# First pairs of parts on VectorE, a six-chunk part first, squares on ScalarE, and output remainders off GpSimd

## What is computed

```python
def rmsnorm(x, g):
    y = x32 * lax.rsqrt(jnp.mean(x32 * x32, axis=-1, keepdims=True) + NORM_EPS)
    return (y * g).astype(x.dtype)

def swiglu(h, w_in, w_out):
    a, b = jnp.split(h @ w_in, 2, axis=-1)
    return (jax.nn.silu(a) * b) @ w_out

x = x + 0.5 * swiglu(rmsnorm(x, g_ffa), w_ffa_in, w_ffa_out)
```

## Time and profile before

| | us |
|---|---|
| median of 3 runs | 2741.33 (2737.09 to 2744.72) |
| the profiled execution | 2743.89 |
| its span, first to last instruction | 2742.2 |
| mean granted TensorE clock | 0.963 |

### The profile page before, as it was taken

One profiled execution on the slowest core, in us unless ns is written; L12 is line 12 of the kernel. 1 busy time (PEld: TensorE's weight loads), 2 busy tenths in 40 slices (PEclk: granted clock), 3 DMA queues, 4 the chain that ended last, 5 costly groups with the idle time before them and its releaser, 6 DMA issues.

```text
span 2742.2 us, 45352 instructions
## 1 busy us (share of the span) xinstructions
PE 2528.1 (92%) x17541; PEld 2395.5 (87%) x17541; DVE 1713.1 (62%) x2326; ACT 1023.4 (37%) x1707; POOL 694.6 (25%) x416
## 2 busy tenths in 40 slices
PE   4999998999899899999997999998999989999988
PEld 4999988876688899898986989898987889898978
DVE  6827367788554883645778637278334696372786
ACT  4525242344233352433234425252134244252422
POOL 2040322212330503223232140503322321405032
PEclk9999999999899999999998999999999999999998
DMA  3323223122232133222222323233323223232322
GB/s 98 92 77 92 83 83 81 41 50 78 67 111 60 54 93 90 79 82 79 80 66 72 92 72 97 62 91 79 93 54 97 81 77 93 76 92 62 91 72 65
DMA packets 410793, 216.25 MB, mean 79 GB/s; under 512 B 40085, under 2 KB 407834, under 8 KB 410650
## 3 DMA queue, kind: packets, MB, share of 16 engines
q1 hardware_dynamic: 404646, 209.17, 27.4%
q0 software_dynamic: 3584, 1.84, 0.4%
q10 hardware_dynamic: 2420, 3.37, 0.4%
HBM read 206.57 MB, written 7.76 MB: 78 GB/s over the span
## 4 chain that ended last, share of the span: by engine, by line
PE 71%; DVE 14%; issue 5%; POOL 5%; ACT 4%; DMA 1%; DVEq 0%; SPq 0%; ACTq 0%; POOLq 0%
PE ps L2431 11%; PE ps L2433 11%; PE ps L2432 11%; PE ps L2374 9%; PE ps L2379 9%; PE ps L2376 9%; PE ps L995 2%; DVE x L2193 1%; DVE st L613 1%; DVE xh L2080 1%; PE ps L909 1%; POOL g2f L1753 1%; POOL wlo L1740 1%; DVE ub L2191 1%; DVE r L2059 1%
## 5 line engine op out<-in xcount | busy, mean ns | idle before, releaser
L1729 POOL TENSOR_TENSOR wlo<-raw,whi 128x1024 fp32r<-128x1024 f32 (+2 forms) x175 | 404.4, 2311 | 1648.8 <-ACT whi L1804 1648.8
L1804 ACT ACTIVATE whi<-raw 128x1024 fp32r<-128x1024 f32 (+2 forms) x175 | 169.5, 968 | 534.6 <-PE ps L2379 509.9
L2374 PE MATMUL ps<-uh,whi 128*128 128x320 f32 (+1 forms) x1408 | 304.5, 298 | 17.8 <-DVE x L2193 10.9
L2376 PE MATMUL ps<-ul,whi 128*128 128x320 f32 (+1 forms) x1408 | 302.8, 296 | 0.0
L2379 PE MATMUL ps<-uh,wlo 128*128 128x320 f32 (+1 forms) x1408 | 302.7, 296 | 0.0
L2191 DVE TENSOR_TENSOR ub<-ps,r 128x576 f32<-128x576 f32 x96 | 72.5, 755 | 298.1 <-PE ps L2379 298.1
L2374 PEld LDWEIGHTS ps<-uh,whi 128*128 128x128 f32 x1408 | 217.3, 190 | 21.9 <-ACT whi L1804 15.7
L2116 DVE TENSOR_TENSOR wlo<-raw,whi 128x1024 fp32r<-128x1024 f32 x76 | 101.0, 1329 | 191.9 <-ACT whi L1820 191.9
L2376 PEld LDWEIGHTS ps<-ul,whi 128*128 128x128 f32 x1408 | 217.3, 190 | 0.0
L2379 PEld LDWEIGHTS ps<-uh,wlo 128*128 128x128 f32 x1408 | 217.2, 190 | 0.0
L2374 PE MATMUL ps<-xh,whi 128*128 128x320 f32 x752 | 167.0, 304 | 16.2 <-DVE xl L2073 8.4
(11 more groups left out here) (430 smaller groups left out, 7394.4 us busy)
## 6 DMA issues: line engine op xcount, KB each, us to landing
raw<-in_w_ffa_in SPq DMA_DIRECT2D x88, 512.0 KB
raw<-in_w_ffb_in SPq DMA_DIRECT2D x88, 512.0 KB
raw<-in_w_ffa_out SPq DMA_DIRECT2D x32, 512.0 KB
pages<-in_cache_ckv SPq DMA_DIRECT2D x128, 128.0 KB, 2.0
raw<-in_w_ffb_out SPq DMA_DIRECT2D x32, 512.0 KB
raw<-in_w_mlstm_in SPq DMA_DIRECT2D x24, 512.0 KB
raw<-in_w_ple_gate SPq DMA_DIRECT2D x16, 512.0 KB
raw<-in_w_ffa_out SPq DMA_DIRECT2D x16, 384.0 KB
```

The lines of the kernel that those rows point to most:

```text
L1729: pool.tensor_tensor(lo[:, 0:n, :], raw[:, p % RAW, 0:n, :], hi[:, 0:n, :].bitcast(F32), ALU.subtract).then_inc(wlo_ready, 1)
L1804: act.activation(hi[:, 0:n, :], raw[:, p % RAW, 0:n, :], ACT.Copy).then_inc(whi_ready, 1)
L2374: mm(out[:, t], hi[:, n, :], xh_n[:, t], start=first and n == 0, stop=False)
L2376: mm(out[:, t], hi[:, n, :], xl_n[:, t], start=False, stop=False)
```

## The change

- `PARTS` becomes 6, 8 and 8 pairs.
- Pair 0 of every part is prepared like the others, by VectorE with `second_sums`, `third_sums` and the four `_lower` functions, placed between the output tiles of the part before (tiles 4, 5 and 6 of `ffn_out`), between the mixer's tiles, the ple's chunks or the chunks of the start. ScalarE's uppers move accordingly. GpSimd's `first_pair` and the semaphores `first_sum` and `first_lo` go.
- Of the output panels, GpSimd makes the remainders of 0 and 1; VectorE those of 2 to 7, in `ffn_out`, behind each tile.
- In the last part ScalarE makes `xh` (a scaled copy) and the squares; VectorE makes `xl` and `acc`.
- In the blocks of x ScalarE scales x (into `xTf` or `xBh`), and VectorE's subtractions multiply by the gain themselves; `gneg` holds negated gains.
- TensorE's output tile waits for the reading of the tile two before (`out_read`) instead of its addition to x.
- The silu of an FFN's pair 0 goes behind the first copy of pair 1; at the start the five squares go between the copies of pair 0.

```diff
-PARTS = [(0, 8), (8, 16), (16, 22)]
+PARTS = [(0, 6), (6, 14), (14, 22)]
...
             def ffn(f):
                 for part in PART[f]:
-                    first_pair(part)
-                    for k in range(8):
+                    for k in (0, 1):
                         lower(part.p + k, 0, part.n)
...
+            def gate(part, i):
+                g = part.g0 + i
+                act.wait_ge(w_act, 2 * g + 2)
+                if g:
+                    act.wait_ge(w_ub, g)
+                act.activation(sA[:, :], tA[:, :], ACT.Silu).then_inc(silu_done, 1)
...
                         copied(part, i, 1, 1, B, A)
+                        if i == 1 and part.q == 0:
+                            gate(part, 0)
...
                     upper(part.p + 1, 0, part.n)
-                    for k in range(2, 8):
-                        upper(part.p + k, 0, part.n)
                     if part.q < 2:
-                        first_pair(PART[f][part.q + 1])
+                        after = PART[f][part.q + 1]
+                        for k in range(2, 8):
+                            if k == 7:
+                                second_upper(after, 0)
+                                third_upper(after, 0)
+                            upper(part.p + k, 0, part.n)
+                        fourth_upper(after, 0)
+                        first_upper(after, 0)
                     else:
-                        upper(part.p + 8, 0, last_upper)
+                        for k in range(8):
+                            if k < 6:
+                                upper(part.p + 2 + k, 0, part.n)
+                            elif k == 6:
+                                upper(part.p + 8, 0, last_upper)
+                            act.wait_ge(tile_taken, part.t + k + 1)
+                            x_scaled_upper(nxt, k)
+                            x_squares(nxt, k)
...
+            def x_scaled_upper(name, c):
+                g = gn[:, GCOL[name] + c:GCOL[name] + c + 1]
+                dst = xh2 if name[0:3] == "ple" else xh
+                act.activation(dst[:, c, :], x[:, c, :], ACT.Copy, scale=g).then_inc(xh_act, 1)
...
+            def panel_lower(p, n):
+                hi, lo = whi[:, p % SPLIT, :, :], wlo[:, p % SPLIT, :, :]
+                dve.wait_ge(wlo_ready, p - 8)
+                dve.wait_ge(whi_ready, p - 7)
+                dve.tensor_tensor(lo[:, 0:n, :], raw[:, p % RAW, 0:n, :], hi[:, 0:n, :].bitcast(F32),
+                                  ALU.subtract).then_inc(wlo_ready, 1)
...
+                for c in range(NC_D):
+                    dve.wait_ge(panel_used, part.p + c + 1)
+                    dve.wait_ge(tile_taken, part.t + c)
+                    dve.tensor_tensor(ub[:, :], slot(part.t + c, bank), r[:, :], ALU.mult).then_inc(out_read, 1)
+                    dve.wait_ge(out_read, NC_D * part.k + c + 1)
+                    dve.scalar_tensor_tensor(out=x[:, c, :], in0=ub[:, :], scalar=-0.5, in1=x[:, c, :], op0=ALU.mult,
+                                             op1=ALU.add).then_inc(tile_taken, 1)
+                    if c < 6:
+                        panel_lower(part.p + 2 + c, part.n)
+                    if name:
+                        if c:
+                            x_sum(name, c - 1)
+                        dve.wait_ge(tile_taken, part.t + c + 1)
+                        x_scaled_lower(name, c)
+                    if c == 4 and after:
+                        second_sums(after, 0)
+                        third_sums(after, 0)
+                    if c == 5 and after:
+                        second_lower(after, 0)
+                        third_lower(after, 0)
+                    if c == 6 and after:
+                        fourth_lower(after, 0)
+                        first_lower(after, 0)
...
+            def x_second(f, k):
+                dve.wait_ge(x_lo, 16 * f + k + 1)
+                dve.scalar_tensor_tensor(out=xTf[:, k, 2, :], in0=x[:, 4 + k, HT:T], scalar=g, in1=xTf[:, k, 2, :],
+                                         op0=ALU.mult, op1=ALU.subtract).then_inc(x_f, 1)
...
             def added(name, f):
                 clear_acc()
+                part = PART[f][0]
                 for c in range(NC_D):
...
                     x_blocks(f, c)
+                    if c == 5:
+                        second_sums(part, 0)
+                        third_sums(part, 0)
+                    if c == 6:
+                        second_lower(part, 0)
+                        first_lower(part, 0)
+                third_lower(part, 0)
                 for k in range(4):
                     x_third_lower(f, k)
+                fourth_lower(part, 0)
...
+                    part = PART[2][0]
+                    second_sums(part, 0)
+                    third_sums(part, 0)
+                    first_lower(part, 0)
+                    second_lower(part, 0)
                     blocks_of(7, p0 + 15, t0 + 17)
+                    third_lower(part, 0)
...
-                    with pe.Fori(0, NC_D // 2) as i:
+                    out_tile(0, 0, lambda n: pe.wait_ge(u_ready, part.g0 + n + 1))
+                    out_tile(1, 0)
+                    with pe.Fori(1, NC_D // 2) as i:
                         for k in (0, 1):
-                            pe.wait_ge(tile_taken, part.t + k - 1 + i * 2)
+                            pe.wait_ge(out_read, NC_D * part.k + k - 1 + i * 2)
+                            out_tile(k, i * 2)
```

More of the change, by code:

```diff
@@ L148, in hybrid_step @@
         gn = whole.put("gn", [P, NG])
+        gneg = whole.put("gneg", [P, 4, 4])
         cf = whole.put("cf", [P, NCF])
@@ L1644, in load @@
                     sp.dma_start(dst, src).then_inc(raw_ready[s], inc)
-            def pair_load(part, i, v):
-                h = 2 * part.half(i)
-                for s in (0, 1):
-                    col = s * FF + (part.a + i) * P
-                    sp.dma_start(raw[:, h + s, :, :], v[:, :, col:col + P]).then_inc(raw_ready[h + s], UNIT)
-            def lowered(part, i):
-                if i:
-                    sp.wait_ge(g_lo, part.remainders(i, 4))
-                else:
-                    sp.wait_ge(first_lo, part.lowered(0, 4))
             def ffn(f, w_in, w_out):
@@ L1662, in ffn @@
                         h = 2 * part.half(i)
[L1663 to L1671 removed]
+                        if f == 0 and part.q == 0 and i == 0:
+                            continue
+                        if i >= 2:
+                            sp.wait_ge(g_lo, part.lowered(i - 2))
+                        for s in (0, 1):
+                            last = max([p for p in range(8, part.p) if p % RAW == h + s], default=0)
+                            if i < 2 and last:
+                                sp.wait_ge(wlo_ready, last - 7)
+                            col = s * FF + (part.a + i) * P
+                            sp.dma_start(raw[:, h + s, :, :], vi[:, :, col:col + P]).then_inc(raw_ready[h + s], UNIT)
                     for k in range(8):
@@ L1861, in ffn @@
                         A, C, B, D_ = [ps[:, part.bank(i) + k, 0:HT] for k in range(4)]
+                        embed = not part.k and not i
                         if i:
@@ L2128, in fourth_lower @@
             def fourth_lower(part, i):
-                dve.wait_ge(g_hi, 4 * (part.g0 + i) + 4)
+                dve.wait_ge(g_hi, part.uppers(i, 4))
                 dve.tensor_tensor(blocks(g4l), raw_pair(part, i)[:, 3, :], blocks(g4h).bitcast(F32),
@@ L2475, in pair @@
                     touch(b + 1)
-                pe.wait_ge(g_hi, 4 * g + 3 + dyn * 4)
-                if first and not e:
-                    pe.wait_ge(first_lo, part.lowered(0, 3))
-                else:
-                    pe.wait_ge(g_lo, part.remainders(e, 3) + dyn * 4)
+                pe.wait_ge(g_hi, part.uppers(i, 3) + add)
+                pe.wait_ge(g_lo, part.remainders(i, 3) + add)
                 pe.wait_ge(w_copied, 4 * g + 1 + dyn * 4)
                 block_product(g3h[:, e, :, :], g3l[:, e, :, :], 0, lambda n: xTh[:, n, 2, :], lambda n: xTl[:, n, 2, :], B,
-                              False, False, need(5, 2))
+                              False, False, need(6, 2))
                 block_product(whi[:, s, :, :], wlo[:, s, :, :], 4, lambda n: xBh[:, n, 0:HT], lambda n: xBl[:, n, 0:HT], A,
-                              False, True, need(6, 2))
+                              False, True, need(5, 2))
                 if new and f:
@@ L2492, in pair @@
                               False, True)
-                pe.wait_ge(g_hi, 4 * g + 4 + dyn * 4)
-                if first and not e:
-                    pe.wait_ge(first_lo, part.lowered(0, 4))
-                else:
-                    pe.wait_ge(g_lo, part.remainders(e, 4) + dyn * 4)
+                pe.wait_ge(g_hi, part.uppers(i, 4) + add)
+                pe.wait_ge(g_lo, part.remainders(i, 4) + add)
                 pe.wait_ge(w_copied, 4 * g + 4 + dyn * 4)
```

303 lines of the change are left out of this document (129 added, 174 removed).

## The result

The changed kernel took 2570.68 us (median of 4 runs, 2569.43 to 2572.78) against 2741.33, a ratio of 0.938 (95% interval 0.936 to 0.940): 170.7 us less. The direction and most of the mechanisms named held; the size was short by 21 us, and the step that failed is the tile time of 6.40 us that I carried over unchanged.

A forecast was written before the change was run, and what follows sets the result against it. TensorE, busy 92%, was taken as the bound, with only its 214 us idle and low-clock stretches winnable. Gains of 81 + 36 + 33 = 150 us from 2743.9 gave 2594, as a median 2592, range 2572 to 2632.

The forecast's parts named there:

- the clock against which all must fit: Output tiles: 6.40 us for eight chunks and 4.80 for six, the time into which all VectorE work must fit.
- the ends: Ends of the four networks: 39.6 us lost before; short part first and work on ScalarE gain 36 us.
- first pairs of parts 1 and 2: Eight places: preparing the pair under the previous part's last tiles saves 10.1 us each, 81 us.
- starts, silu moved: Network starts: the reciprocal comes earlier and the silu of pair 0 moves, together 33 us gained.
- remainders of panels 2 to 7: Output tiles: moving these from GpSimd to VectorE gains nothing by itself, covered by VectorE's slack.
- the margins in the six-chunk part: Part 0's last tiles: panel 7's remainder ends 1.4 us early, the pair's last at 7T + 4.3, 0.5 us early.
- the queue at the starts: Two networks behind a mixer: VectorE's queue puts the reciprocal 17.0 us after the last mixer tile, 7.1 gained each.
- more comes back: Rival, chance 0.06: preparing pair 1 lies in gaps of VectorE's queue at three starts, 19 us more, 2573.
- Pair 0's raw slots come free when panels 4 and 5 are lowered: Loads for the next part's first pair: slots free at 3T + 2.8 and 4T + 2.8, in time for the sums.
- my third rival: Chance 0.03: the next pair's raw lands late, VectorE stands at the sums; 18.8 us late makes 2742, no change.
- The rule against it: Skill advice to move work off a saturated VectorE (84% busy in the first end window); tiles would end later.
- the moved silu: Behind pair 1's first copy, it moves TensorE's wait one product on: 0.7 us gained per network.

The follow-up runs named there:

- a_late: Changed kernel with VectorE preparing the first pairs of parts 1 and 2 only behind the last tile of the part before: 2654.07 us.
- a_pool: Changed kernel with the remainders of output panels 2 to 7 back on GpSimd: 2580.77 us.
- a_start: Changed kernel, first pair of the two networks behind a mixer prepared after the last mixer tile's blocks of x, not between the mixer's tiles: 2578.65 us.
- a_silu: Changed kernel with the silu of each network's pair 0 back behind pair 0's last copy: 2574.47 us.
- b_uh64: Kernel before with an unused tile of 64 bytes per partition between xl and uh: 2730.59 us.
- b_pad64: Kernel before with an unused tile of 64 bytes per partition behind gn: 2724.48 us.
- a_f3: Changed kernel; in the fourth network only, panel 0's upper goes behind the last pair's last copy and the next pair 0's sums one tile later: 2561.36 us.
- a_best: Changed kernel; in the fourth network only, panel 0's upper goes behind the last pair's third copy and the next pair 0's sums one tile later: 2558.84 us.

## Where the prediction held, and which step fell short

The measured 2570.68 us lies below the range. The step that failed is "the clock against which all must fit": a tile's time was taken as the same before and after, so that the place of the operands had no term. It is worth 10.6 to 14.3 us of the 21; the ends, under-sized by 8, come next.

| step | predicted | measured |
|---|---|---|
| first pairs of parts 1 and 2 | 81 | 82: 20.2, 20.8 and 20.0 in the first three networks, 20.3 predicted (the fourth counted as the second); 82.8 lost in `a_late` |
| network ends | 36 | 44: 10.9, 11.3 and 10.7 in the first three |
| starts, silu moved | 33 | about 37: 11.9 at the very start, 2 x 6.4, 6.9 to 8.7, and 4.8 inside the networks |
| remainders of panels 2 to 7 | 0 | 8.5 to 9.5 if taken back (`a_pool`), already in the rows above |
| place of the operands in SBUF | not seen | 10.6 to 14.3 |
| fourth network, raw late | not seen | -8.5: 13.3 us over the second network (7.6 before ScalarE's upper, 4.8 in the tiles, 1.0 of half clock), 4.8 before |

82 + 44 + 37 + 12.5 - 8.5 = 167, within 4 us of the two measurements, 170.7 and 167.4 (2738.73 - 2571.32).

- **Right: first pairs.** The time behind the last tile, its half clock and the margins in the six-chunk part (0.6 us where I had 0.5) came as worked out. The margin was partly luck: my own terms, added again, put the last remainder at about 7T + 4.6, not 4.3, which leaves 0.2 us.
- **Right: the queue at the starts.** 17.7 us behind the last mixer tile for 17.0; `a_start` shows that the preparation does not lie in gaps. So my second rival, "more comes back", had the size (2573) but not the mechanism: it was that gaps would hide the preparation of pair 1.
- **Wrong: "the clock against which all must fit".** I took a tile's 6.40 us as the same before and after, in every stage. The diff has a new tile, `gneg`, 64 bytes in front of nearly all operands, and I read it as a VectorE matter. It moved the matmuls' moving operands by 64 bytes and took 3 to 4 ns from the spacing of each 320-column one, start to start. A six- or eight-chunk tile became shorter by 0.06 or 0.08 us, 10.6 to 14.3 us in all. This step had no term at all; it is more than half of the 21 us.
- **Wrong in size: the ends.** I took what TensorE lost as idle time and clock from the earlier trace rows. For the second network the windows gave 10.2 us lost. By the tile starts the same short part took 50.59 us against 38.87, 11.7 lost, of which a later reciprocal gives back 0.4. I think that the windows count matmuls as work that are stretched, but did not test it. And of the 3.6 us that I let remain, the tiles show nothing. The way to measure such a loss is by intervals of the product, not by an engine's busy time.
- **Wrong: the raw slots.** "Pair 0's raw slots come free when panels 4 and 5 are lowered" holds in three networks. In the fourth they are 5 and 6, and my third rival (raw late, 0.03) came true there, at 4.4 us in the six-chunk part. The larger share, ScalarE's wait for panel 0 inside the last pairs, was in no rival. I had checked one network and multiplied by four.
- **Put at nothing: the remainders.** I looked for a wait of TensorE for GpSimd in the kernel before, found none among the costly ones and wrote 0. In the new order GpSimd would be late in the six-chunk part (13.6 us of waits against 3.5), so moving them is a condition of the rest, worth 8.5 to 9.5 us.
- **Small, and right by luck: the pair with the reciprocal.** I gave the moved silu 0.7 us a network, and `a_silu` lost 3.2 for all. But at full clock it is 0.17 each. The second and third network gained 1.7 and 1.6, because the half clock behind the stop inside pair 1 went (below).
- **The rule against it.** "Perfetto Trace Analysis" of the Trainium skill, "Optimizing Scalar/DVE Operations", says that with VectorE saturated it may make sense to move some of its work to ScalarE or even GpSimd. I left out that it goes on to say that GpSimd might not help, as the two share a read port. The trace fits both halves: `xh` and the squares went to ScalarE, GpSimd's remainders came onto VectorE, and at the ends VectorE is now busy 141 us of 230, where it had 50 of 60 in the first window. A part of that share had been stretched operations, which `a_pool` shows coming back (1219 to 1393 ns, 907 to 1695 ns). "SBUF — State Buffer" of the Trainium skill, "Who interferes with whom", says that a VectorE operation with two SBUF inputs contends with a GpSimd operation that reads SBUF; `g3l` and `acc` are such, and agree. The row that I had cited for it, `xh`, has only one tensor as input, so it was the wrong witness.

What stays open: 4 us of scatter in the mixer of layer 0 (470.8 to 475.0 us from reciprocal to reciprocal, in kernels with the same code there), and the share of ScalarE's scaling in the starts, which was not tried alone.

## What to carry to other kernels

Ask of every wait whether the work could be issued under the stage before, and of every stage boundary in which slot or phase it begins: a schedule that fits three stages can miss in the fourth because of one odd panel. When a change adds or removes a tile, print the addresses before and after: where the moving operand starts can be a cost of its own, and a pad is a one-line experiment. Measure what a stage loses by the intervals between its products as well as by busy time: the two gave 11.7 and 10.2 us for the same network end.

## What the hardware showed that I had not expected

**Where the moving operand starts.** A matmul of 320 fp32 columns took 312 to 313 ns with its operand at the old place and 307 to 310 ns with it 32 or 64 bytes further; start to start 149 and 144 to 146 (groups of 64 to 704 matmuls, those with many at half clock left out; the same picture in six kernels). By the sizes of the tiles ahead of them the old places are multiples of 128 bytes behind the start of `x`; the address of `x` itself stands in no run. A tile of 48 matmuls (320 and 256 columns in turn) shrinks by 0.08 us, and the kernel has (1408 + 752 + 128 + 128 + 96 + 64) x 3 = 7728 of them: an estimate of 161 x 0.08 = 12.9 us, between the 10.6 and the 14.3 measured. Pairs of 288 columns react otherwise: 11.15 us with all tiles at 0, 11.14 at 64, 11.18 at 32, and 11.11 in `b_uh64`, where only part of their operands moved. Why was not tried.

**A short stop and the clock.** In the second network of the kernel before TensorE stopped for 2.04 us inside pair 1 and ran the next stretch at 0.57 of its clock, mostly 1.2 instead of 2.4 GHz; in `b_pad64`, with the same code, the stop at this place was 1.64 us and the clock stayed at 1.00. The rows of the two, a timeline row and the window behind it for each:

```profile
973.46 0.37 PE L2431 MATMUL ps<-xTh,g3h 128*128 128x288 f32 x1 [2.04 <-ACT ps L1851]
...
974.00:978.00 4.00, 4.00 (x21) 4.00 (x20) 2.57 (x4) 2.91 (x5) 0.00 (x0) 0.57 0.66 191
```

```profile
966.08 0.37 PE L2432 MATMUL ps<-xTh,g3h 128*128 128x288 f32 x1 [1.64 <-ACT ps L1852]
...
967.00:971.00 4.00, 4.00 (x32) 4.00 (x32) 2.77 (x4) 2.65 (x5) 0.00 (x0) 1.00 0.77 212
```

It ran 21 matmuls in 4 us in the one and 32 in the other. The reciprocal to the fourth silu took 39.58 and 38.03 us: 1.55 us, of which the stop itself is 0.40.

It looks like a rule on the stop's length. In the five kernels with this order there are 15 such stops behind the first network: the seven of 1.60 to 1.65 us were all followed by full clock, the eight of 2.04 to 2.47 us all by half clock. The changed kernel and its variants say that length doesn't decide alone. Of their 21 stops of 1.74 or 1.75 us, 14 were followed by full clock and seven by half clock, which cost 1.0 us, 38.83 instead of 37.86 to the fourth silu (in the second network, whose code is the same, the stop of 1.75 us kept full clock in `a_f3` and lost it in `a_best`). `a_silu` has 2.48 us in three networks, with half clock behind it in two and full clock in the third:

```profile
917.54 0.58 PE L2456 MATMUL ps<-xTh,g3h 128*128 128x288 f32 x1 [2.48 <-ACT ps L1803]
...
918.00:922.00 4.00, 4.00 (x24) 4.00 (x24) 2.57 (x4) 2.93 (x5) 0.00 (x0) 0.70 0.61 178
```

```profile
1392.49 0.37 PE L2456 MATMUL ps<-xTh,g3h 128*128 128x288 f32 x1 [2.48 <-ACT ps L1803]
...
1393.00:1397.00 4.00, 4.00 (x32) 4.00 (x32) 2.57 (x4) 2.85 (x5) 0.00 (x0) 1.00 0.63 181
```

What else decides is not shown. So a difference of about 1 us a network between two traces here can be the clock and not the edit.
